# Two first units of a stage on unnormed input: MLPs and key stage of a fused two-block network

## The reference, cut to what matters

```
def rms_norm(x, g):
    return x * rsqrt(mean(x * x, -1) + EPS) * g
def modulate(x, shift, scale):
    return x * (1 + scale) + shift

h = h + g1 * y
hn = modulate(rms_norm(h, norm2_g[layer]), sh2, sc2)
h = h + g2 * (square(relu(hn @ w1)) @ w2)              # layer 0 and layer 1
hn = modulate(rms_norm(h, kv_norm_g), shift, scale)     # after layer 0
k, v = split(hn @ kv_w, 2)
k = rms_norm(k.reshape(.., 16, 64), k_norm_g)
```

## Time and profile before

| | |
|---|---|
| median of 3 runs | 2598.12 us (2597.91 to 2599.34) |
| profiled execution | 2598.2 us |
| its span | 2596.4 us |
| mean granted clock of PE | 0.981 |
| PE busy | 2498.5 us, 96% |
| DVE busy | 1442.5 us, 56% |
| ACT busy | 1123.8 us, 43% |

### The profile page before, as it was taken

How to read it: one execution, slowest core, us unless ns; L and a number is a source line. 1 busy time by engine, 2 the same in 40 slices (tenths; PEclk the granted TensorE clock), 3 DMA queues, 4 the chain that set the end, 5 groups by cost and what they waited for, 6 DMA issues and landing times.

```text
span 2596.4 us, 32501 instructions
## 1 busy us (share of the span) xinstructions
PE 2498.5 (96%) x12134; PEld 1980.1 (76%) x12134; DVE 1442.5 (56%) x2237; ACT 1123.8 (43%) x1991; POOL 41.8 (2%) x28
## 2 busy tenths in 40 slices
PE   5998999999999899999999999999999999999998
PEld 3886788888776678888887777778878777777886
DVE  6778665556656644433356644454455664455445
ACT  4565434323535534423444534443354554444243
POOL 2000000000000000000000000000010000000001
PEclk7999999999999989999999999999999999999999
DMA  5435366656221112222232122222222121122222
GB/s 233 154 106 192 136 215 200 210 202 212 79 95 50 58 65 99 98 98 97 93 110 73 58 73 69 74 78 83 105 81 106 66 73 66 61 82 74 93 101 102
DMA packets 77901, 280.35 MB, mean 108 GB/s; under 512 B 8640, under 2 KB 8896, under 8 KB 77504
## 3 DMA queue, kind: packets, MB, share of 16 engines
q1 hardware_dynamic: 60624, 218.02, 23.4%
q10 hardware_dynamic: 17136, 60.37, 6.9%
HBM read 276.26 MB, written 2.10 MB: 107 GB/s over the span
## 4 chain that ended last, share of the span: by engine, by line
PE 89%; DVE 6%; ACT 2%; issue 1%; DMA 0%; ACTq 0%; SPq 0%; DVEq 0%
PE ps L220 25%; PE ps L222 24%; PE ps L221 24%; PE ps L1711 2%; PE ps L1798 2%; PE ps L1771 1%; PE ps L1614 1%; PE ps L1715 1%; PE ps L1133 1%; DVE wl L215 1%; PE ps L1671 1%; PE ps L486 1%; ACT wh L212 1%; PE ps L487 1%; PE ps L491 1%
## 5 line engine op out<-in xcount | busy, mean ns | idle before, releaser
L215 DVE TENSOR_TENSOR wl<-raw,wh 128x1024 fp32r<-128x1024 f32 x374 | 459.1, 1227 | 710.6 <-ACT wh L212 710.6
L220 PE MATMUL ps<-xh,wl 128*128 128x512 f32 x1744 | 698.5, 400 | 15.8 <-DVE wl L215 11.9
L222 PE MATMUL ps<-xh,wh 128*128 128x512 f32 x1744 | 682.3, 391 | 0.0
L221 PE MATMUL ps<-xl,wh 128*128 128x512 f32 x1744 | 681.8, 391 | 0.0
L212 ACT ACTIVATE wh<-raw 128x1024 fp32r<-128x1024 f32 x374 | 394.9, 1056 | 656.1 <-PE ps L222 628.8
L220 PE MATMUL ps<-bh,wl 128*128 128x512 f32 x1158 | 458.4, 396 | 12.7 <-DVE wl L215 6.5
L221 PE MATMUL ps<-bl,wh 128*128 128x512 f32 x1158 | 452.1, 390 | 0.0
L222 PE MATMUL ps<-bh,wh 128*128 128x512 f32 x1158 | 452.0, 390 | 0.0
L220 PEld LDWEIGHTS ps<-xh,wl 128*128 128x128 f32 x1744 | 328.7, 188 | 134.1 <-issue 45.8
L222 PEld LDWEIGHTS ps<-xh,wh 128*128 128x128 f32 x1744 | 328.7, 188 | 70.3
L221 PEld LDWEIGHTS ps<-xl,wh 128*128 128x128 f32 x1744 | 329.2, 189 | 66.1 <-issue 1.4
(11 more groups left out here) (316 smaller groups left out, 2556.2 us busy)
## 6 DMA issues: line engine op xcount, KB each, us to landing
raw<-in_w SPq DMA_DIRECT2D x388, 512.0 KB, 3.2
bA<-in_ada ACTq DMA_DIRECT2D x74, 512.0 KB, 4.5
bC<-in_ada SPq DMA_DIRECT2D x9, 512.0 KB, 10.9
bD<-in_ada ACTq DMA_DIRECT2D x8, 512.0 KB, 4.5
bS<-in_ada ACTq DMA_DIRECT2D x8, 512.0 KB, 4.8
bS<-in_attn_bias ACTq DMA_DIRECT2D x8, 512.0 KB, 3.2
bC<-in_ada ACTq DMA_DIRECT2D x6, 512.0 KB, 4.1
bD<-in_ada SPq DMA_DIRECT2D x5, 512.0 KB, 14.9
```

Source lines behind the costliest of these rows:

```text
L215: e.tensor_tensor(wl[p][:], raw[p][:], wh[p][:].bitcast(F32), ALU.subtract)\
L220: e.matmul(out, wl[p][:, blk, 0:M], xhi, start=start, stop=False)
L221: e.matmul(out, wh[p][:, blk, 0:M], xlo, start=False, stop=False)
L222: return e.matmul(out, wh[p][:, blk, 0:M], xhi, start=False, stop=stop)
```

## The change: what it does

At the three boundaries (into MLP 0, the key stage, MLP 1) the gain is 1 + scale times the norm's weight, and it is now made before the stage begins, together with the shift rounded into a high and a low half (`shift_halves`, `shf`). For this the columns of the modulation are loaded in another order, scales first. While the stage before still runs, `ahead` and `ahead_low` make `xh` and `xl` from h times gain, without root and shift. The split of the last unit's successor goes in front of the last tile's square.

`pair_ahead` takes the place of `rstd_of`, `normed` and `first_pair`. Units 0 and 1 run on the unnormed tiles. The shift's contribution to them is a product of its own: the same weights, low and high, with the two columns of `shf`, 16 matmuls for each unit, into banks 4 and 5; DVE adds the two columns to a bias (`sm[:, SB + q]`). The sums and the spread of the root stand between matmuls of the pair. Then all 8 normalized tiles are made in place for the units from 2 on, with the half splits of units 2 and 3 between them, and the spread root is copied to `bC[:, 10]`. The result of unit 0 or 1 is multiplied with that copy on DVE, and gets the bias on ACT: with relu in the MLPs, with the identity in the key stage, where the square is then made from this result and no longer from the bank.

```
+            def pair_ahead(s, u0, used, i, c, n):
+                def tile(q, kt):
+                        ...
+                        need(f"{s}ahi{kt}")
+                        e.matmul(ps[q][:], wl[p][:, kt, :], xh[:, kt, :], start=kt == 0, stop=False)
+                        e.matmul(ps[q][:], wh[p][:, kt, :], xh[:, kt, :], start=False, stop=False)
+                        need(f"{s}alo{kt}")
+                        mm = e.matmul(ps[q][:], wh[p][:, kt, :], xl[:, kt, :], start=False, stop=kt == KD - 1)
+                        ...
+                def shift_column(q):
+                    if pe:
+                        ...
+                        for kt in range(KD):
+                            e.matmul(ps[4 + q][:, 0:2], wl[p][:, kt, :], shf[:, i, kt, :], start=kt == 0, stop=False)
+                            mm = e.matmul(ps[4 + q][:, 0:2], wh[p][:, kt, :], shf[:, i, kt, :], start=False, stop=kt == KD - 1)
+                        done(mm, f"{s}b{q}")
+                    ...
+                def tile_two():
+                    for q in range(2):
+                        tile(q, 2)
+                for q in range(2):
+                    shift_column(q)
+                    for kt in range(2):
+                        tile(q, kt)
+                rstd_of(s, KD, D, bTk, (lambda: None, tile_two))
+                for kt in range(3, KD):
+                    for q in range(2):
+                        tile(q, kt)
+                if dve:
+                    need(s + "rstd")
+                for k in range(KD):
+                    if act:
+                        if k == KD // 2 - 1:
+                            need(f"{s}half1")
+                        elif k == KD - 1:
+                            e.wait_ge(s_unit, u0 + 2)
+                        else:
+                            need(f"{s}pt{k}")
+                    normed_tile(s, k, hk, lambda k: gs[:, n, k:k + 1], lambda k: mod[:, c + k:c + k + 1], xh, bTk)
+                    if k:
+                        put_lo(s, k - 1, bTk, lambda k: mod[:, c + k:c + k + 1], xh, xl)
+                    if k in (1, 2):
+                        split_first(u0 + 1 + k, s, k - 1)
+                    if k == KD - 2:
+                        split_second(u0 + 2)
+                put_lo(s, KD - 1, bTk, lambda k: mod[:, c + k:c + k + 1], xh, xl)
+                split_second(u0 + 3)
+                if dve:
+                    done(e.tensor_copy(bC[:, 10, :], ps[7][:]), s + "spread")
+                    need(s + "spread")
```

In `mlp`:

```
                         if i == 0:
-                            first_pair(u0, b, s + "n", xh, xl)
+                            pair_ahead(s + "n", u0, b, i_sh, c_sh, n_gs)
...
                         if i < 2:
-                            split_second(u0 + 2 + q)
+                            if dve:
+                                e.tensor_tensor(bS[:, q, :], ps[bk][:], bC[:, 10, :], ALU.mult).then_inc(s_bank[bk], 1)
...
-                            if act:
+                            if act and i < 2:
+                                e.wait_ge(s_bank[bk], used + 2)
+                                need(f"{s}nbias{q}")
+                                done(e.activation(bS[:, q, :], bS[:, q, :], ACT.Relu, bias=sm[:, SB + q:SB + q + 1]), f"{s}relu{q}")
+                                need(f"{s}relu{q}")
+                            elif act:
```

In the key stage:

```
             def head_sums(j):
                 if pe:
-                    e.wait_ge(s_bank[j % 4], BK[j % 4] + 1)
-                    if j > 1:
+                    if j < 2:
+                        need(f"K{j}sq")
+                    else:
+                        e.wait_ge(s_bank[j % 4], BK[j % 4] + 1)
...
+                if dve and j < 2:
+                    unit_read(u0, 0, j)
+                    e.tensor_tensor(bC[:, j, :], ps[bk][:], bC[:, 10, :], ALU.mult).then_inc(s_bank[bk], 1)
+                if act and j < 2:
+                    e.wait_ge(s_bank[bk], BK[bk] + 2)
+                    need(f"KVbias{j}")
+                    done(e.activation(bC[:, j, :], bC[:, j, :], ACT.Identity, bias=sm[:, SB + j:SB + j + 1]), f"K{j}out")
+                    need(f"K{j}out")
+                    done(e.activation(squares(j), bC[:, j, :], ACT.Square), f"K{j}sq")
```

More of the change, by code:

```diff
@@ L904, in program @@
                         ada_load(5 * KD + k, pair_of_slots(bA, 2 * k), k)
[L905 to L909, removed]
+                if j == 3:
+                    if dve:
+                        need("nada7")
+                        done(ada_bias(4 * KD, KD), "mod2")
+                        need("mod2")
+                    mod_gain("M0n", 1, 4 * KD, v("norm2_g", 0, 8))
+                if j == 8:
+                    if dve:
+                        need("nada15")
+                        done(ada_bias(3 * KD, KD), "mod3")
+                    if act or dve:
+                        need("mod3")
+                    shift_halves("M0n", 0, 3 * KD)
             U[0] += KW
@@ L919, in h_ready, with mlp @@
                         e.wait_ge(s_bank[b], BK[b] + 1)
-            def mlp(s, g2, ada0, nxt, between, early=None):
+            MOD_ORDER = [0, 7, 6, 1, 2, 3, 4, 5]
+            def mlp(s, g2, ada0, nxt, between, early, i_sh, c_sh, n_gs):
                 u0, b = U[0], list(BK)
                 ada_seen = [16 * n for n in AD]
-                for q in range(2):
-                    split_first(u0 + 2 + q, s + "n", q)
+                mod_col = lambda a: ada0 + 9 * MOD_ORDER[a // 9] + a % 9
                 for c in range(N_FF):
@@ L1003, in mlp, with key_modulation @@
                 root_table(nxt)
[L1005 to L1015, removed]
+            def key_modulation(c, n):
+                if (c, n) == (1, 0):
+                    if dve:
+                        need("M00mod1")
+                    mod_gain("KV", 2, 104, v("kv_norm_g", 0, 8))
+                if (c, n) == (2, 0):
+                    if act or dve:
+                        need("M01mod0")
+                    shift_halves("KV", 1, 96)
+            mlp("M0", 40, 40, "KV", key_modulation, (lambda k: gs[:, 2, k:k + 1], xh, xl), 0, 24, 1)
             def copy_out(bank, used, dst):
@@ L1354, in program @@
             NB[0] += KD
+            gain4 = lambda k: gs[:, 4, k:k + 1]
             u0, b = U[0], list(BK)
@@ L1380, in program @@
                                            ALU.mult, ALU.add).then_inc(s_bank[bk], 1)
+                if n == KD - 1:
+                    split(u0 + 2, 0, n)
                 square("M1n", n, hk(n), bTk(n), lambda: e.wait_ge(s_bank[bk], used + 2))
+                ahead("M1n", n, gain4, xh, xl)
                 if n >= 2:
                     add_square("M1n", n - 1, bTk)
-                    if dve or (act and end):
-                        split(u0 + 2, 0, n)
+                if n:
+                    ahead_low("M1n", n - 1, gain4, xh, xl)
+                if n == KD - 1:
+                    ahead_low("M1n", n, gain4, xh, xl)
+                if 2 <= n < KD - 1 and (dve or (act and end)):
+                    split(u0 + 2, 0, n)
             U[0] += KD
```

103 lines of the change are left out of this document (73 added, 30 removed).

## The result

The changed kernel is slower: 2614.53 us, median of 4 runs (2611.91 to 2617.29), against 2598.41 (2597.91 to 2599.34) for the kernel before on the same chip, ratio 1.006, 95% interval 1.0046 to 1.0074. The forecast was 2613.0 and "slower". The profiled execution took 2617.29, the slowest of the four, with a span of 2615.5.

A forecast was written before the change was run, and what follows sets the result against it. PE, busy 96% of the span, bounds the kernel, with DVE nearly equally loaded at the boundaries. 2.7 + 2.4 + 6.1 + 1.8 + 0.8 + 0.8 + 0.2 = +14.8 on 2598.2 gives 2613.0; range 2603 to 2623.

The forecast's parts named there:

- PE's new order: Before the root at each boundary, PE runs two-column matmuls at 0.106 each, ordinary ones and sums; root 2.7 later.
- B: At each boundary, the slot where the old stage's last matmul ends, taken as zero: 289.47, 648.64, 960.88 before the change.
- rival (c): Lower clock sets in already during the pair of units 0 and 1, some 5 per boundary: 2628; chance 0.08.
- floor of 25 ns: Matmul-to-matmul minimum; by it the 32 two-column matmuls would cost 0.8 instead of 3.4, forecast 5.4 lower, 2607.6.
- DVE's chain: DVE's list after R takes 15.8; unit 2 stops after four k-tiles until R + 13.1; of PE's 5.0, 0.9 is left.
- R: Moment the root is there at a boundary, from which DVE makes normalized tiles; forecast B + 10.3, 2.7 later than before.
- rival (a): PE alone decides each boundary because DVE and ACT keep up: -5.0, -5.2, -6.1, so 2581.9; chance 0.07.
- Unit 4: In both MLPs its weight split queues behind units 0 and 1's results, ready at B + 35.4: +2.7 and +2.4.
- rival (b): Units 0 and 1's results don't hold up unit 4: -0.9 and -1.2 in MLPs, +7.9 key stage, 2604; chance 0.05.
- Key stage: Head sums in front of unit 2 wait for ACT's square; PE idles 12.2, unit 2 starts at B + 29.5: +6.1.
- The clock: Lower clock behind PE's waits: 1.8 in the key stage after 12 idle us, 0.8 in each MLP.
- The start: Before MLP 0, early tiles push unit 10's low weights in the recurrent output projection past their time: +0.2.

The follow-up runs named there:

- Experiment 2: The changed kernel with unit 4's split put ahead of units 0 and 1's results in ACT's and DVE's lists of both MLPs: 2611.71 us, ratio 1.0048.
- Experiment 1: The changed kernel with the key stage's head sums 0 and 1 moved in PE's list to before unit 3's seventh k-tile: 2606.66 us, ratio 1.0031.
- second trace: The changed kernel itself, unaltered, run again in another group beside the kernel before: 2612.84 us, ratio 1.0057.
- experiment 8: Experiment 6's kernel with only the order of the pair's tiles changed as in experiment 7, DVE's list left alone: 2606.03 us, ratio 1.0026.
- experiment 7: Experiment 6's kernel with the pair's tiles in another order and DVE's list of norm, low parts and splits laid out by hand: 2587.62 us, ratio 0.9956.
- experiment 6: Experiment 3's kernel with two-column matmuls beside their tiles and DVE's work on their result behind its norm list: 2598.04 us, ratio 0.9997.
- experiment 4: The changed kernel with the shift's two-column matmuls for one k-tile instead of eight: 2607.35 us, ratio 1.0032.
- experiment 3: The changed kernel with the edits of experiments 1 and 2 together: 2602.95 us, ratio 1.0015.

## Why the prediction was right, point by point

- **PE's new order.** A two-column matmul took 0.107 to 0.112: the 16 from 291.08 to 292.79 make 1.71, where 1.70 stood. The root came at B + 10.6, forecast 10.3, at all three boundaries, and the pair was through at B + 17.3, forecast 16.8. The granted clock was 1.00 throughout, which rules out rival (c) for this kernel. The Trainium skill's floor of 25 ns ("TensorE: Matmul & The Clock Gate", section "Wait — 56ns, not 53.3ns?") is not what set the pace of these matmuls, at 0.107 each; the one-column row was the right guide.
- **DVE's chain.** Unit 2's fifth k-tile was to start at R + 13.1 and did at R + 12.9, after a wait of 3.01 (forecast 3.4) at MLP 0, and likewise at MLP 1. This is what rules out rival (a): DVE's list ended 15.7 behind R (316.75 and 0.61 more; forecast 15.8), not 9.
- **Unit 4.** Its weights were forecast at B + 35.4, and it started at B + 35.5. Experiment 2 shows the cause, the results of units 0 and 1 in front of the split, and with it that rival (b) was wrong. The wait was 2.03, not 3.6: PE arrived later, slowed by the clock behind the first wait, as the text said, but the list of what the profile would show forgot it.
- **Key stage.** The wait was 11.79, forecast 12.2, released by ACT's square. The sums started at B + 29.2, where R + 18.7 made it B + 29.0. Experiment 1 takes the wait away and with it 6 to 8 us.
- **The clock** was the term sized least well. Behind the key stage's wait it cost 2.8 in one trace and 1.7 in another (forecast 1.8). In MLP 0 it decides between +4.6 and +3.0, a cost of 1.6 or of nothing, where 0.8 was forecast: in the second trace the clock stayed low longer behind unit 2's wait, PE came to unit 4 later, the wait there was 0.62 and the clock didn't fall again (below, timeline and stretch of the second trace). In the first it was 2.03, and the clock fell (0.53 between 328 and 330, as shown above). Unit 4 started at B + 35.5 both times. In MLP 1 it did not fall behind the wait for unit 4, so the 0.8 there was one too many, and the stage cost 2.9 instead of 3.2. That the sum of the three clock terms (3.4) lies between what the two traces show (4.4 and 1.7) is in part luck: the parts were off one by one. Of the 4.5 by which the two traced executions differ, 1.6 lie in MLP 0 and 1.1 behind the wait of the key stage.

```profile
326.16 0.50 PE L221 MATMUL ps<-xh,wl 128*128 128x512 f32 x1 [0.62 <-DVE wl L216]
```

```profile
328.00:330.00 2.00, 2.00 (x11) 1.65 (x10) 1.17 (x2) 1.94 (x4) 0.00 (x0) 1.00 0.94 305
```

- **The start.** +1.6 and +1.1 before MLP 0 were forecast as 0.2. The kernels above have the same code up to there and show -0.3 to +2.1, while their first weight unit already starts between 59.5 and 61.2, against 59.8 before. Without that difference -0.1 to +0.7 is left, and 0.6 and 0.5 for the change, where 0.2 was forecast. So the larger part is the spread of the program's start and not the change; with one trace of the kernel before, the rest can't be given to the change for certain.

The forecast terms add up to +14.8; the medians say +16.1 and, in the second group, +14.0.

Two figures of the forecast don't follow from its own working. Its upper sum of +27 is 2625, above the 2623 at which the range ends. And rival (b)'s 2604 is 5.8 over the kernel before, more than the 5.2 within which it is counted as "same". The measured time lies clear of both.

## What to carry to other kernels

Work ahead on unnormed input takes away PE's waits only if everything queued behind the late root is laid out again: here the 4.5 to 4.8 us that PE had gained in each MLP when unit 2 began were given back because DVE had the norm in front of unit 2's second half of weights, and ACT and DVE served results before the weights of unit 4; in the key stage what was won was lost again because PE had a reduction in its list in front of work that was ready. Before such a change, write down for each engine what stands behind the delayed value and who wants it first; the same idea then turned from +0.6% to -0.4%. An order on PE and the lists of the engines that overwrite its input belong together: the new order alone cost 8.0 us (experiment 8), and with the lists laid out for it, it brought 10.4 (experiment 7 against 6).

## What the runs showed of the hardware

- Waits of nearly the same length had different ends. Behind the 3.01 in unit 2 the clock fell to about 0.50 in both MLPs of the change, while behind 3.02 in MLP 1 of experiment 4, and behind 3.01 in the key stage of experiments 3 and 8, it stayed at 1.00. One of 2.03 in MLP 0 of the change brought it down, one of 1.95 in MLP 1 did not. Behind the 0.98 to 1.09 of experiment 6 it stayed at 1.00. The low stretches lasted from 3 to 6 us of matmuls in traces of the same code, and in the key stage the same wait cost 2.0 us of clock in experiment 1 and nothing in experiment 3. So a clock term of such a wait is good to a microsecond or two a place.
- Sixteen one-column sums between full matmuls left the clock at 1.00 in the change, but it stood at 0.50 for a while at the same sums or the spread in MLP 1 of experiment 6, in MLP 0 and the key stage of experiment 7 and in MLP 0 and MLP 1 of experiment 8, with no wait before them in experiment 7. What parts these cases stays open.
